# Sample index scores and their top-k search moved into the first mixer periods of a one-core decoder-trunk kernel

## The reference, cut to what matters

```python
def index_scores(iq, ik, iw):
    s = jnp.einsum('bthd,bsd->bths', iq.astype(F32), ik.astype(F32)) * IDX_DIM ** -0.5
    return jnp.einsum('bths,bth->bts', jax.nn.relu(s), iw.astype(F32))

def dsa_sample(q, k_new, v_new, iq, ik_new, iw, cache_k, cache_v, cache_kidx, page_table, topk):
    ...
    sc = jnp.where(vis, index_scores(iq, ik_all, iw), -jnp.inf)
    _, sel = lax.top_k(sc, topk)
    ...
    return sparse_attend(q, kg, vg, ok)
```

## Time and profile before

| | us |
|---|---|
| median of 3 runs | 3923.28 (3912.94 to 3934.06) |
| the profiled execution's own time | 3918.59 |
| its span in the profile | 3917.0 |
| mean granted TensorE clock | 0.918 of full |

### The profile page before, as it was taken

One profiled execution on the slowest core, in us unless ns is written; L12 is line 12 of the kernel. 1 busy time (PEld: TensorE's weight loads), 2 busy tenths in 40 slices (PEclk: granted clock), 3 DMA queues, 4 the chain that ended last, 5 costly groups with the idle time before them and its releaser, 6 DMA issues. The chain is left out here.

```text
span 3917.0 us, 47867 instructions
## 1 busy us (share of the span) xinstructions
PE 3315.8 (85%) x15513; PEld 1829.7 (47%) x15513; DVE 1872.0 (48%) x3884; ACT 1387.3 (35%) x2843; POOL 860.7 (22%) x1709
## 2 busy tenths in 40 slices
PE   7996888898888886776376999999999928988998
PEld 4553344444444443443233444444455526655665
DVE  0000146678787877433910151432513646764664
ACT  2210136666666675740111112111121124442442
POOL 3322323222111110000000000000000027772772
PEclk9998999999999997787688999999999959998999
DMA  6656766554333330003305112111110132224221
GB/s 185 180 168 194 238 204 191 154 159 137 120 111 114 105 94 20 4 4 109 163 6 230 65 33 75 35 59 55 33 69 23 38 122 87 98 87 124 76 82 60
DMA packets 254617, 402.42 MB, mean 103 GB/s; under 512 B 46900, under 2 KB 131933, under 8 KB 251773
## 3 DMA queue, kind: packets, MB, share of 16 engines
q1 hardware_dynamic: 229568, 370.27, 29.2%
q10 hardware_dynamic: 20736, 21.05, 1.6%
q0 software_dynamic: 4096, 8.40, 0.9%
HBM read 318.01 MB, written 102.89 MB: 107 GB/s over the span
## 5 line engine op out<-in xcount | busy, mean ns | idle before, releaser
L602 PE MATMUL PB<-wb,hT_ahead 128*128 128x512 f32 x1088 | 549.0, 636 | 55.9 <-DMA hT_ahead<-out_hT_all 40.7
L1925 PE MATMUL QB<-hT,w_c 128*128 128x512 f32 x1024 | 449.4, 593 | 0.0
L602 PEld LDWEIGHTS PB<-wb,hT_ahead 128*128 128x128 f32 x1088 | 199.3, 201 | 278.8 <-issue 219.8
L613 PE MATMUL PT<-ident,sm 128*128 128x128 f32 x1088 | 193.5, 302 | 130.9 <-ACT sm L741 128.5
L1925 PEld LDWEIGHTS QB<-hT,w_c 128*128 128x128 f32 x1024 | 190.0, 190 | 217.1 <-issue 217.1
L300 PE MATMUL P0A<-w_all,hT 128*128 128x512 f32 (+1 forms) x816 | 266.6, 487 | 0.0
L613 PEld LDWEIGHTS PT<-ident,sm 128*128 128x128 f32 x1088 | 132.1, 151 | 265.1 <-ACT sm L741 155.6
L2630 PE MATMUL RPJ<-w_co,oT 128*128 128x512 f32 x544 | 249.9, 609 | 4.2 <-ACT oT L2814 3.2
L1894 PE MATMUL QA<-w_c,hT 128*128 128x512 f32 (+1 forms) x768 | 249.7, 481 | 3.4 <-DVE crow L2199 2.3
L749 ACT COPY ptT<-PT 128x512 f32<-128x512 f32 (+3 forms) x320 | 164.5, 519 | 244.0 <-PE PT L613 243.5
L1868 PE MATMUL QS<-w_o,yT 128*128 128x512 f32 x544 | 238.9, 597 | 6.0 <-ACT yT L2055 6.0
(11 more groups left out here) (415 smaller groups left out, 5237.5 us busy)
## 6 DMA issues: line engine op xcount, KB each, us to landing
wb<-in_w_in_ab SPq DMA_DIRECT2D x272, 512.0 KB, 3.9
out_c_all<-crow SPq DMA_DIRECT2D x256, 64.0 KB, 1.6
out_pr_all<-pr_out SPq DMA_DIRECT2D x17, 546.0 KB, 3.7
pra<-out_pr_all SPq DMA_DIRECT2D x16, 546.0 KB, 4.7
x_rows<-in_x_all SPq DMA_DIRECT2D x17, 512.0 KB, 5.8
out_hT_all<-hT SPq DMA_DIRECT2D x17, 512.0 KB, 2.9
hT_ahead<-out_hT_all SPq DMA_DIRECT2D x17, 512.0 KB, 3.7
yab<-out_yab_all SPq DMA_DIRECT2D x17, 512.0 KB, 5.0
```

The costliest lines, as they stand in the source:

```text
L602: ins = pe.matmul(PB[:, :], hT[:, 2 * q + k, :], wb[:, u % 4, k, :], start=(q == 0 and k == 0), stop=(q == 3 and k == 1))
L613: ins = pe.transpose(PT[v % 2][:, k * P:(k + 1) * P], sm[:, 2 * (r % 2) + a, c * CH + k * P:c * CH + (k + 1) * P], ident[:, :])
L1925: ins = pe.matmul(PB[b % 2][:, 0:N], w_c[:, c, b * P:(b + 1) * P], hT[:, c, 0:N], start=(c == 0), stop=(c == KD - 1))
```

## The change

**Samples' index part.** Scores, search and mask of the 32 sample rows leave `layer0_samples` and become steps of `layer0_mixers` in the places -380 to -5 (`sample_steps`). The work borrows tiles that the mixers do not need yet (rows of `isc`, `sm`, `ptT`). Index keys are loaded 1 MB at a time and turned in 16 units of four blocks, evicted by ACT and DVE in turn. The search is done by sign sums on ACT instead of counts on DVE. The mask goes to memory (`mb_s`) and the samples' stage loads it.

**Samples' stage.** The first two key loads come at the stage's start, ahead of the constants; the retention gets its own tiles and its steps lie between the four key turnings; keys are evicted by ACT and DVE in turn; the second values' load comes when all keys are turned, the first when the states are stored.

**Mixers.** For g < 6 the projection's rows alternate between `hT_ahead` and a free half of `vst`, and are loaded earlier; for g < 4 the projection alternates between the banks `PB` and `PO`; the constants are loaded after the first rows and three weight pieces, and PE waits for them only at its first turning.

**Conv stage.** The conv state is loaded right after the first rows, before `w_o`; the first input rows come between the halves of `w_o`; `w_c` is loaded by SP (one part behind `w_o`, the other behind the first stores and loads of rows), not by ACT.

```diff
@@ mixers_order
-            add(b - (83 if f else 150), "sp", "load", f)
+            add(b - (83 if f else 101), "sp", "load", f)
...
-            add(b - 5, "sp", "load_h", g)
+            add(b - (60 if g <= TWO_H else 5), "sp", "load_h", g)
...
+def sample_steps(add):
+    add(-380, "sp", "s_load")
+    add(-317, "pool", "s_rope")
+    add(-316.5, "pool", "s_select")
+    add(-316, "pe", "s_turn")
+    add(-315, "dve", "s_spread")
+    for c in range(SCH):
+        p = -310 + 22.0 * c
+        if c < SCH - 1:
+            add(p - 9, "sp", "s_stage", c)
+            for i in range(HB):
+                add(p + 3 * i, "pe", "s_blocks", c, i)
+                add(p + 3 * i + 1, ("act", "dve")[i % 2], "s_copy", c, i)
+        add(p + 12, "pe", "s_index", c)
+        add(p + 13, "act", "s_relu", c)
+        add(p + 16, "pe", "s_weight", c)
+        add(p + 17, "dve", "s_score", c)
+    add(-204, "dve", "s_bounds")
+    for k in range(STEPS):
+        add(-203 + 8.0 * k, "act", "s_signs", k)
+        add(-203 + 8.0 * k + 1.6, "act", "s_side", k)
+        add(-203 + 8.0 * k + 3.2, "act", "s_move", k)
+    add(-8, "dve", "s_rank")
+    add(-5, "sp", "s_store")
...
+            return vst[:, 8:16, :] if g < TWO_H and g % 2 else hT
+            return PO if g < FILL and n % 2 else PB
...
+            def s_signs(k):
+                if k == 0:
+                    act.wait_ge(S["s_middle"], after(1))
+                else:
+                    act.wait_ge(S["s_moved"], after(k))
+                act.activation(signs[0:SR, :], s_row, ACT.Sign, bias=s_mid, scale=1.0, accum_out=s_cnt)
...
+            def s_bounds():
+                dve.wait_ge(S["s_scored"], after(SCH))
+                link(dve.tensor_reduce(s_lo, s_row, AX, ALU.min))
+                link(dve.tensor_reduce(s_hi, s_row, AX, ALU.max))
...
+            def s_rank():
+                dve.wait_ge(S["s_moved"], after(STEPS))
...
+                dve.tensor_scalar(s_row, tie, BIG, -BIG, ALU.mult, ALU.add).then_inc(S["s_mask_ready"], 1)
...
+            def s_store():
+                sp.wait_ge(S["s_mask_ready"], after(1))
+                sp.dma_start(io["mb_s"][:, :], s_row).then_inc(S["s_mask_stored"], 16)
@@ layer0_samples, sync
-                index_in(i)
+                keys_in(i)
...
             sp.wait_ge(S["zeroed5"], after(3))
+            sp.dma_start(mb128[0:SR, :], io["mb_s"][:, :]).then_inc(S["mb4"], 16)
...
             for i in range(2, HB):
-                sp.wait_ge(S["kt_ps"], after(4 * (i - 1)))
-                index_in(i)
+                sp.wait_ge(S["kt_ps"], after(8 * (i - 1)))
+                keys_in(i)
@@ layer0_samples, tensor
+            keys(0)
...
+            keys(1)
...
+            ret_add(0)
+            ret_add(1)
+            keys(2)
+            ret_add(2)
+            ret_add(3)
+            keys(3)
@@ layer0_samples, vector
+            evac_keys(0)
...
+            evac_keys(1)
+            spread_v(0)
+            spread_v(1)
+            dve.wait_ge(S["ro4_ps"], after(1))
+            state_add(0)
+            spread_v(2)
+            state_add(1)
+            spread_v(3)
+            evac_keys(2)
+            state_add(2)
+            state_add(3)
...
-            for n in range(STEPS):
-                link(dve.tensor_scalar(mb[:, :], isc[:, :], mid, 0.0, ALU.is_gt, ALU.add, accum_out=cnt))
...
+            evac_keys(3)
@@ layer0_out_and_conv
-            sp.dma_start(xin[:, :], io["x_all"][0:P, :]).then_inc(S["x2_loaded"], 16)
+            sp.dma_start(crw[0:DB * 3, :], io["state_conv"]).then_inc(S["pre_loaded"], 16)
...
+            for c in range(KD):
+                sp.dma_start(w_c[:, c, CC:CIN], io["w_in_c"][c * P:(c + 1) * P, CC:CIN]).then_inc(S["w2z_loaded"], 16)
...
-            act.wait_ge(S["w2o_loaded1"], after(16 * KD))
-            for c in range(KD):
-                act.dma_start(w_c[:, c, CC:CIN], io["w_in_c"][c * P:(c + 1) * P, CC:CIN]).then_inc(S["w2z_loaded"], 16)
```

More of the change, by code:

```diff
@@ L662, in _ @@
                     turn_o(*which)
+                elif name == "s_turn":
+                    s_turn()
+                elif name == "s_blocks":
+                    s_blocks(*which)
+                elif name == "s_index":
+                    s_index(*which)
+                elif name == "s_weight":
+                    s_weight(*which)
                 else:
@@ L782, in _ @@
                     copy_o(*which)
+                elif name == "s_copy":
+                    s_copy(*which)
+                elif name == "s_relu":
+                    s_rectify(*which)
+                elif name == "s_signs":
+                    s_signs(*which)
+                elif name == "s_side":
+                    s_side(*which)
+                elif name == "s_move":
+                    s_move(*which)
                 else:
@@ L974, in _ @@
                     gn_mean(*which)
+                elif name == "s_spread":
+                    s_spread()
+                elif name == "s_copy":
+                    s_copy(*which)
+                elif name == "s_score":
+                    s_score(*which)
+                elif name == "s_bounds":
+                    s_bounds()
+                elif name == "s_rank":
+                    s_rank()
                 else:
@@ L1159, in _ @@
                     store_yb(*which)
+                elif name == "s_load":
+                    s_load()
+                elif name == "s_stage":
+                    s_stage(*which)
+                elif name == "s_store":
+                    s_store()
                 else:
@@ L1403, in _, with keys, ret_add @@
             turned = [0]
-            for i in range(HB):
+            def keys(i):
                 pe.wait_ge(S["stage%d" % (i % 2)], after(16 * (i // 2 + 1)))
-                turn([index_block(i, 4 * q + k) for q in range(4) for k in range(4)])
+                turn([stage[:, i % 2, 4 * q + k, P * g:P * (g + 1)] for g in range(2) for q in range(4) for k in range(4)])
+            def ret_add(h):
+                pe.wait_ge(S["vm4"], after(h + 1))
+                pe.wait_ge(S["rs4_upd"], after(2 * h))
+                for g in range(2):
+                    pe.matmul(PS[g][:, :], kd[:, h, :],
+                              vm[:, h % 2, 4 * g:4 * g + 4, :].rearrange("p b d -> p (b d)"), start=True, stop=True)\
+                      .then_inc(S["su4_ps"], 1)
+            keys(0)
             pe.wait_ge(S["qkb4"], after(1))
@@ L1592, in _ @@
             dve.wait_ge(S["q4_ps"], after(2))
-            for n in range(3):
+            for n in range(2):
                 src = PO[0][:, n * P:(n + 1) * P].rearrange("p (r t) -> p r t", t=SR).unsqueeze(1)\
@@ L1686, in _ @@
-            link(dve.scalar_tensor_tensor(band, order, need, band, ALU.is_le, ALU.mult))
-            link(dve.tensor_tensor(band, band, above, ALU.add))
-            dve.tensor_scalar(mb[:, :], band, BIG, -BIG, ALU.mult, ALU.add).then_inc(S["mb4"], 1)
+            evac_keys(3)
             for g in range(2):
@@ L1836, in _ @@
             rows_in(2)
+            for c in range(KD):
+                sp.dma_start(w_c[:, c, 0:CC], io["w_in_c"][c * P:(c + 1) * P, 0:CC]).then_inc(S["w2c_loaded"], 16)
             ahead(0, 3)
```

394 lines of the change are left out of this document (236 added, 158 removed).

## The result

The changed kernel took 3825.89 us (median of 4 runs, 3822.07 to 3831.68) against 3924.27 for the kernel before (4 runs beside it): ratio 0.9754, 95% interval 0.9728 to 0.978. The profiled execution took 3825.2 us, 93.4 less than the one before; the sum on record was 90 less. By stretches, from the first load of each stage: the mixers end 32.7 us later (1807.04 against 1774.4; predicted 25), the samples' stage reaches its attention 103.1 us sooner (predicted 100), from there to the conv stage it is 2.1 sooner, and that stage has its first z projection 19.2 us sooner (predicted 15). The sum of these is 91.7.

The account below looks back on a forecast made before the run. The samples' search and ranking stood alone on the path, PE and ACT idle; in the mixers' first periods ACT was free, PE not. Samples -100, mixers +25, conv -15 gave -90 from 3918.59: 3828.6, stated as 3830, range 3796 to 3862.

Parts of the forecast that it names:

- Samples' stage, -100: Samples' stage up to its attention: without search and ranking, first matmul at 1852 instead of 1953.05; 100 us taken, bounds 92 to 106.
- two signs of a wrong prediction: Tile 5 starting within 10 us of 547.6 or after 600; attention starting later than 90 us into the samples' stage.
- The rival that let the stage give only 84: Samples' stage: low clock after transposes, or DVE holding the keys, gives 84 instead of 100; total 3845, chance 0.08.
- Mixers, +25: Mixers' first periods: added index work, search and ranking delay the weight behind the store; mixers end 25 us later, bounds +3 to +50.
- the fill's -31 before tile 2: Mixers up to tile 2's start: earlier start, row waits and bank waits removed, together 31 us less.
- the row waits (-14): Mixers before tile 2: two row waits go, 7 us each with the slow-clock matmuls and turnings behind them.
- the bank waits (-7): Mixers before tile 2: seven bank waits of 0.7 us and a matmul's tail of 0.3 go, 7 us.
- 35 + 12 = 47 on record: Mixers up to tile 2: 32 us for four index-key pieces, 3 for query turnings, 12 for added waits (0 to 25).
- Conv, -15: Conv stage's start: first projection ends near 2085 to 2088 instead of 2102.7; 15 us less, bounds -8 to -18.
- Fits better: Mixers: few PE waits, ACT's copies in the search chain's gaps; mixers only +3, total 3807, chance 0.2.
- Starves: Mixers' fill: index loads and weights share one queue and starve PE; mixers +50, total 3854, chance 0.12.
- Slower: Mixers: search steps stretched to 8.9 us by work between them; mixers +156, total 3960, chance 0.03.

Follow-up runs that it names:

- run 4: Changed kernel with the nine constants loaded ahead of the first two key loads in the samples' stage: 3823.62 us, ratio 0.9751.
- run 12: Changed kernel with search behind ACT's query copies, ranking in six pieces, later store, constants first, last key evictions before the group norm: 3800.6 us.
- run 8: Changed kernel with all the samples' retention steps ahead of the key turning, not interleaved with it: 3834.52 us, ratio 0.9776.
- run 9: Changed kernel with the 24 search steps placed behind the copies of tile 1's queries in ACT's order: 3820.17 us, ratio 0.9738.
- run 1: Changed kernel with the mask's store moved from place -5 to place 60 in SP's order: 3826.26 us, ratio 0.9748.
- Run 10: Kernel before with the fill's edits alone (two row tiles, two banks, constants behind the first weights): 3890.16 us, ratio 0.9917.
- run 6: Changed kernel with one tile for the projection's rows again: 3825.79 us, ratio 0.9743.
- run 7: Changed kernel with one bank for the projection again in tiles 0 to 3: 3824.98 us, ratio 0.9742.
- run 3: Changed kernel with 8 of the 24 search halvings, so its mask differs: 3808.52 us, ratio 0.9705.
- run 11: Changed kernel with 8 of the 24 search halvings and one tile for the projection's rows: 3812.21 us, ratio 0.9719.

## Why the prediction was right, and where it was not

**Samples' stage, -100.** Measured -103.1. Neither of the two signs of a wrong prediction came (tile 5 began at 582.8, between 557.6 and 600; the attention well before 90 us). Each step held: DVE's first eviction 26.5 us after the stage's start (26.6 by the sum), the last state added after 61.2 (63.6), group norm and last keys 14.4 (14). I did not see that two of its waits could be removed by order alone; runs 4 and 12 took 16 us out of the 78 that I had called its length up to the attention.

**The clock.** The rival that let the stage give only 84 did not happen: 1846 to 1867, with turnings between the retention's products, ran at 1.00.

```profile
1827.00:1846.00 19.00, 11.94 (x69) 8.92 (x68) 10.50 (x22) 4.10 (x7) 0.00 (x0) 0.66 0.66 180
1846.00:1867.00 21.00, 17.50 (x114) 12.76 (x111) 11.99 (x15) 2.35 (x4) 0.00 (x0) 1.00 0.28 103
```

In run 8 PE did nothing but turn keys from 1858.88 to 1885, and the clock rose while it did:

```profile
1858.00:1866.00 8.00, 7.10 (x32) 5.67 (x32) 3.25 (x5) 1.76 (x3) 0.00 (x0) 0.55 0.20 37
1866.00:1884.00 18.00, 12.95 (x80) 9.75 (x80) 6.93 (x11) 5.86 (x10) 0.00 (x0) 0.91 0.78 276
```

The Trainium skill (TensorE: Matmul & The Clock Gate, Part 4: PE-mode transpose) says that the full clock does not engage for transposes, as they do not count as busy in the same way. These rows differ from it: with nothing but transposes on PE, the granted clock went from 0.55 to 0.91.

**Mixers, +25.** Measured +32.7. The path that I had named is the right one: index scores, bounds, 24 steps, ranking, store, a weight's landing. Along it the search on ACT, 83 us on record, took 87.8, and it started 2.3 us later than forecast: 7 of the 7.7 us. The cause of the longer search is the order on ACT (run 9: 79.6 us with the same work). The cause that I gave for the last hold, SP's order alone, is half of it: with the store moved away the ranking on DVE holds PE one step later (run 1). Ahead of this path the start gave 6.7 us and not 10: PE's first projection came at 321.18 and not at 317.5.

**The step that failed without being seen in the sum: the fill's -31 before tile 2.** On record the earlier start (-10), the row waits (-14) and the bank waits (-7) all lie before tile 2. Run 10 has 14.9 us there: 9.1 for the start and 5.8 for both kinds of wait, where the record has 21. The rows of before show part of the reason: six bank waits stand up to tile 2 and not seven, and the slow matmuls behind tile 2's row wait, counted in its 7, come after that tile's start. The rest went to other waits: PE stands 8.3 us for weights up to tile 2 in run 10, 1.0 before. The other 15.0 us of run 10 come between tile 2 and tile 5, where the sum had 2. That its 31.4 equal my 31 is luck.

The price of the samples' work up to tile 2 was too large as well: 35 + 12 = 47 on record, 34.0 measured (427.89 less run 10's 393.94). Two terms, 16 and 13 us too large, cancelled, so that the 425 forecast for tile 2 came within 3 us of 427.9; that is luck too.

In the changed kernel the second row tile and the second bank, each taken back by itself, cost nothing that shows (runs 6 and 7). What rows show of why: from 318 to 364 the weights' queue moves 306 GB/s with its engines 0.91 busy (from 364 to 426 only 198 and 0.63); in tile 1 index work stands between the projection steps; and from tile 2 on the samples' chain sets the pace. Tile 5 begins 45.5 us behind the store in the changed kernel, and 45.9, 46.1, 47.4, 46.2, 44.7, 45.4 and 44.9 in runs 3, 4, 6, 7, 8, 9 and 11, whatever PE waited for before. Where both are undone together in the changed kernel, the time was not taken; that stays open, as does how the cover divides between queue and chain.

The mixers of the changed kernel end 65.2 us later than those with the fill's edits alone (1807.04 against 1741.83), where the record has 25 + 31 = 56. Of the 9 us between them, 7.7 are the miss of the +25.

**Conv, -15.** Measured -18, and -19 at the z projection: the upper bound on record. `out_proj(0)` did not have to wait for `w_o` at all (0.68 us for ACT's copy). ACT's issuing of `w_c` stood ahead of its first copy for 10 us (2076.20 to 2086.16). The Trainium skill (DMA: Bandwidth & Descriptors, Issuing engines are not separate DMA queues) says that another issuing engine saves only the sequencer's time; by it the move would be worth those 10 and no more. Order of loads and move together gave 18, and no run separates them. That the order has a part can be seen at PE's turning of the conv state, 20.7 us after the stage's start before and 8.0 after. The transfers' own times changed with it: the median landing of `w_c`'s pieces went from 6.9 to 12.7 us (520 KB) and from 19.3 to 14.1 (1 MB), with other loads beside them.

**Rivals.** "Fits better" (3807) was reached only by changing orders. "Starves" did not happen: between the first index key load (352.44) and tile 2, PE waits for no weight, and for index keys 1.12 and 0.51 us. "Slower" needed 7.2 us a step; the chain had 3.66.

## What to carry to other kernels

Before adding up the waits that an edit removes, find the chain that sets the end of that stretch once all edits are in; a wait beside it has no price, and undoing the edit in the final kernel shows that. Check such a sum at a point inside the stretch as well as at its end: two terms that are both too large can cancel. A serial chain laid over two busy engines costs less than its length, but by its position in an in-order engine it can make its own suppliers late: put copies that another engine waits for ahead of it. And a long block on one engine, with a transfer behind it in an ordered queue, holds twice: here moving the transfer alone took 2.8 us off the way from the search's end to tile 5, and cutting the block as well 5.9.

## What the runs showed of the hardware

The duration of issuing a transfer depends on what is queued already. In the changed kernel the first seven constants behind the two 2 MB key loads took 0.44 to 0.92 us each to issue, and the eighth, of 4 KB, held SP for 6.26 us. Ahead of the keys the same issue took 0.43 (run 4), and the hold moved to the next issues behind them: the states' four took 12.27 us instead of 5.43. So a first few issues behind a large load go out at once and a later one stands, small or not; what fills up is not shown.

```profile
1814.20 6.26 SPq L1578 DMA_DIRECT2D sc<-in_bsel  x1
```

```profile
1811.61 0.43 SPq L1576 DMA_DIRECT2D sc<-in_bsel  x1
...
1813.51 12.27 SPq L1583 DMA_DIRECT2D rows_a<-in_state_ret  x4
```

After an idle of 3 to 4 us PE's next matmuls can run at the lower clock, so that a wait costs more than its bracket says. In run 6 four matmuls took 3.78 us behind 3.67 us of idle (granted clock 0.50 from 428.7 to 432.5), against 1.98; behind 3.81 us they took 2.97 (0.64 from 475 to 478), and behind 3.13 us 2.58.
